# A hybrid encoder layer on one core: the pooling fold, chunk 0's norm and attention, and chunk 1's transposes at other places in the order

## What is computed

```python
def mixer(x, mem, ...):
    h = x @ w_in                                   # 1024 -> 384 + 384 + 384 + 256
    a_val, a_gate, p_in, q = split(h)
    a = a_val * sigmoid(a_gate)
    a = causal_depthwise_conv(a, conv_w, conv_b)   # width 31
    a = silu(layer_norm(a, conv_ln_g, conv_ln_b))
    p = pool_mixer(p_in, pool_w, pool_scale)       # (trailing means over 2/4/8/16 - the frame) @ pool_w, scaled
    mo = memory_cross_attention(q, mem, w_mk, w_mv)  # 4 heads, 256 memory tokens
    return concatenate([a, p, mo]) @ w_out

def reference(x, ...):
    x = layer_norm(x, ln0_g, ln0_b)
    x = layer_norm(ALPHA * x + mixer(x, ...), ln1_g, ln1_b)
    x = layer_norm(ALPHA * x + conv_ffn(x, ...), ln2_g, ln2_b)
    return x
```

## Time and profile before

| | us |
|---|---|
| three timed runs, median | 2089.0 |
| lowest and highest of them | 2088.79, 2092.34 |
| the profiled execution | 2091.08 |
| its span, first to last instruction | 2089.4 |
| PE busy in the span | 1892.1 (91%) |
| DVE, ACT busy | 1480.4 (71%), 942.5 (45%) |
| change of phase, span us | 303 to 315.1 |
| conv pairs | 315.1 to 386.3 |
| pooling pairs | 386.3 to 431.9 |
| fold, chunk 0's norm, last weights | 431.9 to 467.6 |

### The profile page before, as it was taken

The page is one execution under the profiler, slowest core; times in us unless marked ns, Lnnn a source line. Parts: engine busy times, 40 slices in busy tenths (PEclk is TensorE's granted clock), DMA queues, the critical chain, the costliest instruction groups (busy, mean ns, idle before and its releaser), DMA issues.

```text
span 2089.4 us, 26011 instructions
## 1 busy us (share of the span) xinstructions
PE 1892.1 (91%) x8626; PEld 1570.2 (75%) x8626; DVE 1480.4 (71%) x1883; ACT 942.5 (45%) x1598; POOL 242.6 (12%) x335
## 2 busy tenths in 40 slices
PE   4899977659999849999999999999999797999997
PEld 3688867648788738888888778888888686887886
DVE  6444008548898557888888788777778766656898
ACT  3111113445565345655665656555656434324331
POOL 1111002101122200222122002000000000000111
PEclk9899998879999969999999999999999999999999
DMA  5322125452443363343334523222214557557543
GB/s 211 136 91 97 46 65 170 117 180 92 161 142 124 131 238 111 123 148 141 141 122 149 202 101 139 83 90 90 80 70 141 184 204 261 187 176 261 181 161 121
DMA packets 171546, 296.12 MB, mean 142 GB/s; under 512 B 11600, under 2 KB 105936, under 8 KB 171472
## 3 DMA queue, kind: packets, MB, share of 16 engines
q1 hardware_dynamic: 171472, 295.18, 40.5%
HBM read 189.23 MB, written 105.91 MB: 141 GB/s over the span
## 4 chain that ended last, share of the span: by engine, by line
PE 55%; DMA 3%; DVE 3%; issue 1%; ACT 1%; SPq 0%; DVEq 0%; ACTq 0%
PE prod_ps L1858 55%; DVE mov_lo L2040 1%; DMA mov_raw<-x_operands 1%; DMA mov_raw<-wdown_sums_scratch 1%; DMA y_scratch<-up_and_out 1%; ACT mov_hi L1905 1%; DMA mov_raw<-in_w_down 0%; DVE up_and_out L2074 0%; DVE up_and_out L2071 0%; DMA up_and_out<-x_scratch 0%; DVE sta_lo L2036 0%; ACT prod_ps L1912 0%; DVE sta_raw L2052 0%; DVE sta_sums L2050 0%; ACT sta_hi L1898 0%
## 5 line engine op out<-in xcount | busy, mean ns | idle before, releaser
L1858 PE MATMUL prod_ps<-mov_hi,sta_hi 128*128 128x512 f32 x1848 | 727.2, 394 | 44.3 <-ACT prod_ps L1912 24.9
L1858 PE MATMUL prod_ps<-mov_lo,sta_hi 128*128 128x512 f32 x1848 | 725.3, 392 | 0.0
L1858 PE MATMUL prod_ps<-mov_hi,sta_lo 128*128 128x512 f32 x1848 | 724.5, 392 | 0.0
L1858 PEld LDWEIGHTS prod_ps<-mov_hi,sta_hi 128*128 128x128 f32 x1848 | 351.0, 190 | 122.8 <-ACT prod_ps L1912 27.0
L1858 PEld LDWEIGHTS prod_ps<-mov_hi,sta_lo 128*128 128x128 f32 x1848 | 350.7, 190 | 74.1
L1858 PEld LDWEIGHTS prod_ps<-mov_lo,sta_hi 128*128 128x128 f32 x1848 | 350.9, 190 | 72.6
L2036 DVE TENSOR_TENSOR sta_lo<-sta_raw,sta_hi 128x512 fp32r<-128x512 f32 (+1 forms) x340 | 222.8, 671 | 65.1 <-ACT sta_hi L1898 63.2
L1898 ACT ACTIVATE sta_hi<-sta_raw 128x512 fp32r<-128x512 f32 (+1 forms) x340 | 198.1, 611 | 142.2 <-PE prod_ps L1858 103.3
L255 PE MATMUL wb<-x0t_hi,win_hi 128*128 128x512 f32 x352 | 141.2, 401 | 1.4 <-DVE x0t_lo L345 1.4
L255 PE MATMUL wb<-x0t_hi,win_lo 128*128 128x512 f32 x352 | 138.6, 394 | 0.0
L255 PE MATMUL wb<-x0t_lo,win_hi 128*128 128x512 f32 x352 | 138.5, 394 | 0.0
(11 more groups left out here) (248 smaller groups left out, 2680.7 us busy)
## 6 DMA issues: line engine op xcount, KB each, us to landing
sta_raw<-in_w_up SPq DMA_DIRECT2D x88, 512.0 KB, 4.1
hidden_scratch<-up_and_out SPq DMA_DIRECT2D x44, 512.0 KB, 2.6
y_scratch<-up_and_out SPq DMA_DIRECT2D x16, 1024.0 KB, 7.5
sta_raw<-hidden_scratch SPq DMA_DIRECT2D x32, 512.0 KB, 4.7
up_and_out<-y_scratch SPq DMA_DIRECT2D x16, 1024.0 KB, 4.9
x_operands<-x_operands_out SPq DMA_DIRECT2D x56, 256.0 KB, 4.2
mov_raw<-x_operands SPq DMA_DIRECT2D x14, 1024.0 KB, 6.3
mov_raw<-in_w_down SPq DMA_DIRECT2D x44, 256.0 KB, 4.6
```

Source lines behind the costliest of these rows:

```text
L1858: last = pe.matmul(psum, w, x, start=(start and k == 0 and i == 0), stop=(stop and k == m - 1 and i == 2), skip_group_check=True)
```

## The change

In `project_phase`, chunk 1's eight turns stand behind projections 3 to 10 of chunk 0 rather than 1 to 8. For the later chunks nothing moves.

In `mixing_phase`:

- the conv taps come in two loads, four groups first and twenty behind the first pair's input, and are split in two steps;
- keys stand behind pair 3 (was 4) and values behind pair 6 (was 7);
- the fold is done in two halves of three banks (`ps_s` twice, `ps_o`), behind pairs 9 and 11, evacuated by ACT and DVE at pairs 10 and 12; w_out's first three tiles and the pooling weights are split earlier for it;
- softmax of chunk 0 starts one pair later, and `conv_total`, `mean`, `deviations`, `squares`, `square_sum`, `variance`, `deviation`, `scale_conv`, `swish` and `conv_lo` of chunk 0 stand at pairs 17 to 22;
- the pooling pairs use the two banks of `ps_y` alone, since `ps_m` now holds the mean; a pair waits for the evacuation of the pair two before;
- DVE copies the two edge columns (`lead_x`) ahead of the low half, GpSimd reads the copy, and `load_pair` waits for the copy (`edge_x`) rather than for `g_fix`;
- chunk 0's conv rows and chunk 1's query and conv rows are loaded at pairs 13 and 14; behind the last store only the pooling rows of both and w_out's last four tiles remain;
- the wait for all of w_out stands behind chunk 1's first scores and mean.

The core of the diff (`JT - 2 * TT` is 3):

```diff
+        def first_turn(c):
+            return 1 if c else JT - 2 * TT
...
-                    if c + 1 < NCH and 1 <= n <= 2 * TT:
-                        turn(c + 1, n - 1)
+                    first = first_turn(c)
+                    if c + 1 < NCH and first <= n < first + 2 * TT:
+                        turn(c + 1, n - first)
...
+            sp.dma_start(taps[:, tap_cols[0], :], taps_src[:, tap_cols[0], :]).then_inc(gt_in[0], 16)
             load_pair(0)
+            sp.dma_start(taps[:, tap_cols[1], :], taps_src[:, tap_cols[1], :]).then_inc(gt_in[1], 16)
...
                 if m >= 4 + CONV_PAIRS:
-                    sp.wait_ge(g_fix, m - 3 - CONV_PAIRS)
+                    sp.wait_ge(edge_x, m - 3 - CONV_PAIRS)
...
+                if m == 13:
+                    for i, s in enumerate(g_stored):
+                        sp.wait_ge(s, 16 * (CONV_PAIRS // 4 + (i == 0)))
+                    load_chunk(sp, 0, 0, 0, CT, land[2])
+                if m == 14:
+                    sp.wait_ge(prep_lo, 3)
+                    load_chunk(sp, 1, 1, 2 * CT, KT, early1_in)
+                    load_chunk(sp, 1, 1, 0, CT, early1_in)
...
-                if m >= 3:
+                if m >= CONV_PAIRS:
+                    pe.wait_ge(g_out, 2 * m - 2)
+                elif m >= 3:
                     pe.wait_ge(g_out, 2 * m - 4)
...
+                if m == 3:
+                    keys()
+                if m == 6:
+                    values()
+                if m == 9:
+                    fold(0)
+                if m == 11:
+                    fold(1)
+                if m == 13:
+                    pe.wait_ge(fold_lo, 2 * CT)
+                    scores(0, 0)
...
+                if m == 17:
+                    mean(0)
+                if m == 18:
+                    turn(0, 1)
+                if m == 20:
+                    attend(0)
+                    variance(0)
...
+                if m >= CONV_PAIRS:
+                    dve.tensor_copy(lead_x[:, m - CONV_PAIRS, :, :], gx_raw[:, m % 4, :, 0:2]).then_inc(edge_x, 1)
```

More of the change, by code:

```diff
@@ L973, in _ @@
                         for w, x in exact_parts(*rows, wo_hi[:, CT + di, cols], wo_lo[:, CT + di, cols]):
-                            last = pe.matmul(fold_bank[2 * ci + b], w, x, start=(n == 0), stop=(n == 3 * len(ds_) - 1))
+                            last = pe.matmul(fold_bank[ci], w, x, start=(n == 0), stop=(n == 3 * len(ds_) - 1))
                             n += 1
                     last.then_inc(fold_mm, 1)
-            pe.wait_ge(fold_lo, 2 * CT)
+            pe.wait_ge(ident_ok, 3)
+            for m in range(NP):
+                pair(m)
+                if m == 3:
+                    keys()
+                if m == 6:
+                    values()
+                if m == 9:
+                    fold(0)
[4 more added lines that the diff above has]
+                    scores(0, 0)
+                if m == 15:
+                    scores(0, 1)
+                if m == 16:
+                    turn(0, 0)
+                if m == 17:
[5 more added lines that the diff above has]
+                    variance(0)
+            pe.wait_ge(g_out, NG)
+            pe.wait_ge(o_lo, 1)
             def chunk(c, s, before):
@@ L1000, in chunk @@
                     turn_x1(before, 0)
-            mean(0)
-            variance(0)
-            pe.wait_ge(wo_l, KT)
             chunk(1, 1, 0)
@@ L1021, in query_hi @@
                 if isinstance(c, int) and c == 0:
-                    act.wait_ge(q0_in, 16 * TT)
+                    act.wait_ge(land[1], 48)
+                elif isinstance(c, int) and c == 1:
+                    act.wait_ge(early1_in, 16 * 2 * TT)
                 else:
@@ L1169, in _ @@
                     turned_hi(0, 1)
+                    squares(0, 0)
                 if m == 21:
                     attn_hi(0, 0)
+                    deviation(0)
+                if m == 22:
+                    act.wait_ge(land[0], 48)
+                    swish(0, 0)
             wout_hi(3)
[L1173 to L1177 removed]
+            query_hi(1, 1)
+            wout_hi(4)
+            wout_hi(5)
+            pooled_hi(0, 0)
+            wout_hi(6)
+            wout_hi(7)
             def turned_x1(c, u):
@@ L1392, in _ @@
                     prep_low(wk_lo, r_wk, wk_hi, 2)
-                if m == 5:
+                if m == 4:
+                    dve.wait_ge(land[3], 16 * (len(pool_blocks) + 1))
+                    for t in range(CT):
+                        last = dve.tensor_scalar(r_pw[:, t, :], r_pw[:, t, :], psc[:, t:t + 1], None, ALU.mult)
+                    last.then_inc(prep_zero, 1)
                     for t in range(QT):
```

246 lines of the change are left out of this document (117 added, 129 removed).

## The result

| | before | after |
|---|---|---|
| median of the timed runs, us | 2088.89 | 2073.77 |
| lowest and highest | 2087.95, 2092.34 | 2069.57, 2074.88 |
| the profiled execution, us | 2091.08 | 2073.64 |
| its span, us | 2089.4 | 2071.9 |

The change makes the kernel faster by 15.1 us: the ratio is 0.9921, its 95% interval 0.9903 to 0.9939. The forecast was 2073.

A forecast was written before the change was run, and what follows sets the result against it. TensorE, busy for 91% of the 2089.4 us span, was taken as the bound. Terms -11.4 + 15.4 - 21.9 + 1.8 = -16.1 took the profiled 2091.08 to 2075.0; timed runs lie 2.1 lower, so 2073 us, range 2067 to 2079 (0.60).

The forecast's parts named there:

- chunk 1's transposes: Projection phase: two projections fill PE's 14.03 us gap before the first transpose, less a new wait; -11.4 us, bounds -9 and -12.
- start of the conv pairs: Change of phase: a smaller first taps load and less ACT and DVE work start PE sooner; -2.1 us, between 0 and -2.5.
- conv pairs: Conv stage: half the fold joins, with waits on DVE and some half clock; +7.1 us, between +4.1 and +12.
- to the first scores: Behind the last conv group: fold's second half, two pool pairs and emptying its three banks take 9.9 us; +5.2 us.
- scores to attention: Pool pairs: conv sum, mean and deviations join the chain, while ACT's waits for loads go; -0.6 us, bounds -4 and +5.
- attention to last evacuation: End of pool pairs: ACT's last evacuation now stands behind chunk 0's norm, 15.4 us instead of 9.6; +5.8 us.
- tail: Last pool evacuation to first projection: norm and fold gone, last w_out tile sets 13.8 us instead of 35.7; -21.9 us.
- first unit, cold: First 24 projection matmuls: PE, idle for most of the stretch before, starts at half clock; +1.8 us, 0 to 3.
- 60.52 stays: Chunk 1's first transpose keeps its time of 60.52 us, since the norm before it waits for its load, not PE.
- rival b: Last weights late: SP's queue held 4.9 us, softmax and norm chain 4 longer from half-clock waits; 2082 us, chance 0.20.
- (a): Waits between conv pairs covered: no half clock in conv or pool pairs, warm, shorter end stretch; 2063 us, chance 0.13.
- (c): PE between pairs 3 and 13 stays at half clock; with 25 us more of it the time is 2098; chance 0.03.

The follow-up runs named there:

- the fold in existing waits: Changed kernel with the fold's first half behind pair 17, ahead of the conv mean, and its second behind the last pool pair: 2061.34 us, ratio 0.9863.
- swish late: Changed kernel with swish of chunk 0's conv norm and its low half moved behind the last pool evacuation: 2068.23 us, ratio 0.9901.
- swish and weights: Changed kernel with swish and its low half behind the last pool evacuation, and three w_out loads issued among the pool pairs: 2067.9 us, ratio 0.9897.

## Why the prediction was right, and where it wasn't

| term | predicted | measured in the trace |
|---|---|---|
| chunk 1's transposes | -11.4 | -10.2 (105.31 against 115.48) |
| start of the conv pairs | -2.1 | -2.7 (gap 9.57 against 12.27) |
| conv pairs | +7.1 | +5.3 (76.5 against 71.2) |
| to the first scores | +5.2 | +5.7 (10.4 against 4.7) |
| scores to attention | -0.6 | -0.6 (30.7 against 31.3) |
| attention to last evacuation | +5.8 | +5.5 (15.1 against 9.6) |
| tail | -21.9 | -20.4 (15.3 against 35.7) |
| first unit, cold | +1.8 | +2.7 (8.39 against 5.7) |
| sum | -16.1 | -14.7 |

The errors of the single terms lie between -1.8 and +1.5 us and come to 6.8 without their signs, to 1.4 with them. So part of the hit to within 1 us is that they cancelled. Errors of this size mean little for one stage: the conv stage of the old order took 71.1 and 69.5 us in two traces, that of the new one 76.2 to 78.0 in five.

By their own steps:

- **Transposes.** The gap and the new wait came out as worked out (3.17 for 3, 1.46 for 1.2 to 1.7). "60.52 stays" was off by 1.2 us: the norm's load landed later, at 57.01 instead of 55.80. In the traces of the other kernels that carry this same part of the change it moves between 55.62 and 57.09, so this is the start-up, not the change. As a term it was -11.4, and 9.3 us is what it gave alone.
- **Conv pairs.** The waits before keys and values (2.16, 2.15) were predicted at 2.4 and 2.5, that before the fold (1.18) at 1.4. The band waits came differently (4.07, 1.13, 0.69 for 2.7, 1.8, 1.1), with nearly the same sum. All waits were 11.4 for 11.9. The mis-sized part is the half clock: it and small remainders were put at 7.1 and were 5.9 (76.5 less 59.2 of work and 11.4 of waits), since the groups behind 1.13 and 0.69 us ran at full clock (2.05 us each).
- **First scores, and attention.** Each step as costed. ACT waits for no pair's load, as promised. In the pool stage PE's large waits stayed in kind, 4.45 and 8.54 us, the latter now before the mean.
- **The norm's chain.** 15.4 predicted for the way from attention to last evacuation, 15.1 measured. The trace sides with the row and not with the drain that the "ScalarE: Activation LUTs" page of the Trainium skill has (What ACT_TABLE_LOAD costs): the load at 426.21 starts 0.02 us after the end of the copy before it and the root 0.01 us after the load.
- **Tail.** 13.8 was too short by 1.5. I had taken 4.1 us for the landing of the last two w_out tiles; they took 6.4, with the DMA engines busy for 0.92 of that stretch. The prediction had both the 4.1 and the 8.0 of the earlier trace rows and chose the lower; with less ahead in the queue the landing was in between. SP was not held at these loads (rival b): its last two w_out issues took 0.96 us where two took 5.33 before. It was held later, at 446.12, where one issue of a chunk load took 3.38 us, but nothing that the tail waits for stood behind that one.
- **First unit.** 1.8 was 0.9 too small; twelve of the 24 matmuls ran at half clock.
- **After it** the lead is 14.7 us, and the rest of the span's 17.5 appears in the steady chunks and the last phase, where the code is the same. The medians differ by 15.1, so I take it for the difference between two executions. From the start of the first unit to the end the kernel before took 1621.8 us, the kernel after 1621.5, and all eleven traces of this study lie between 1618.4 and 1622.0, which bears this out.

The rivals didn't come. Most of (a)'s conditions were false: there was some half clock, and a cold start. (c) was wide of the mark, with a granted clock of 0.93 in the conv stage.

**What the prediction missed** is in no term. It took 14.2 us of fold and evacuations out of the tail at full price, and charged about 14 for them among the pairs (4.9 and 1.4 there, then 4.8 and 2.9). So it saw the fold as neutral. But once the norm has left the tail of the changed kernel, its length is set by stores and w_out loads, and PE, ACT and DVE idle in it. With the fold in that tail it took 20.0 us, without it 15.3: leaving it earned 4.7 us and not 14.2. Among the pairs the fold cost 9.0 us and not 14. The ladder of ratios shows it: transposes alone 0.9954; all of the change but the fold's new place 0.9887; the whole change 0.9921; the fold in existing waits 0.9863.

## What to carry to other kernels

When a change takes two things out of a stretch, ask what bounds the stretch after the first is gone; the second may then have been cheap where it stood (here 4.7 us and not 14.2). Put filler work into waits that the profile shows on the engine and that other work ends (here 8.5 us for the softmax chain, and 10 for the last loads), not between steps that another engine paces. And look at what the last store or evacuation stands behind in its engine's order: a wait, a table load and swish, 6 us together, ahead of a 0.6 us evacuation cost about 5.

## What the runs showed of the hardware

- The clock after idling: in the kernel after, PE stood still for 8.46 us before the first unit, and 12 of its 24 matmuls came at about 0.43 us each, the other twelve at 0.23. With 9.63 us ahead of it (swish late) the unit took 7.1 us, with 7.33 (swish and weights) 8.2: a longer wait was not a slower start.
- The same 24 attention matmuls behind the same wait of 2.4 us took 3.1 us in five of these kernels and 4.2 to 4.6 in four.
- Moving a load earlier does not make it land earlier by as much: with the evacuation 4.7 us sooner, the first of the last two w_out tiles was converted 2.8 us sooner (swish late against the changed kernel, both counted from the first conv pair).
